# Cross-attention's exponentials one step later, last feed-forward group by token halves, gate tile of 32 columns

## The reference, cut to what matters

```
proj = h @ w_in                       # mixer; g_low has 16 columns
log_g = log_sigmoid(g_low @ gk_w2 + gk_b) / 16

q = (h @ wq).reshape(b, s, 4, 256)    # cross-attention, 4 heads
kv = mem_n @ wkv
scores = einsum('bshd,bmhd->bhsm', q, k) * 256 ** -0.5
probs = softmax(scores)
o = einsum('bhsm,bmhd->bshd', probs, v) ;  return o @ wo

u = conv3(h @ w_up) ; return (silu(gate) * val) @ w_down
out = rms_norm_2(x, norm_final_w)
```

## Time and profile before

| | us |
|---|---|
| median of 3 runs | 2532.43 (2531.82 to 2532.86) |
| profiled execution, whole time | 2531.77 |
| its span, first to last instruction | 2530.2 |
| PE busy | 2472.4 (98%) |
| DVE busy | 1397.4 (55%) |
| ACT busy | 792.6 (31%) |
| POOL busy | 79.1 (3%) |

### The profile page before, as it was taken

One profiled execution on the slowest core, in us unless ns is written; L12 is line 12 of the kernel. 1 busy time (PEld: TensorE's weight loads), 2 busy tenths in 40 slices (PEclk: granted clock), 3 DMA queues, 4 the chain that ended last, 5 costly groups with the idle time before them and its releaser, 6 DMA issues.

```text
span 2530.2 us, 31908 instructions
## 1 busy us (share of the span) xinstructions
PE 2472.4 (98%) x11704; PEld 2047.4 (81%) x11704; DVE 1397.4 (55%) x2254; ACT 792.6 (31%) x1473; POOL 79.1 (3%) x90
## 2 busy tenths in 40 slices
PE   8999999999999999999999999999999999999997
PEld 6868888888788878788788888888888888888886
DVE  5537788777542242335454753463687347734763
ACT  4234444454531121222232242453232112211223
POOL 1000000000000000021000030002000000000000
PEclk9999999999999999999999999999999999999998
DMA  5111111111111131221110042461111111111112
GB/s 194 42 33 42 51 42 51 50 44 57 48 44 50 50 108 50 78 80 55 34 50 21 26 143 63 136 196 50 42 50 50 50 50 50 42 49 50 50 46 79
DMA packets 236688, 157.75 MB, mean 62 GB/s; under 512 B 5087, under 2 KB 225396, under 8 KB 235075
## 3 DMA queue, kind: packets, MB, share of 16 engines
q1 hardware_dynamic: 231632, 133.71, 17.9%
q0 software_dynamic: 3088, 14.54, 1.6%
q10 hardware_dynamic: 1890, 8.43, 1.0%
HBM read 135.69 MB, written 20.97 MB: 62 GB/s over the span
## 4 chain that ended last, share of the span: by engine, by line
PE 92%; DVE 3%; ACT 2%; DMA 1%; issue 1%; SPq 0%; ACTq 0%; DVEq 0%
PE bank L698 27%; PE bank L699 27%; PE bank L700 27%; PE bank L990 1%; PE bank L832 1%; PE bank L991 1%; PE bank L992 1%; DMA wraw<-in_w_in_dram 1%; PE bank L843 1%; ACT whi L1199 1%; PE bank L794 1%; PE bank L844 1%; PE bank L822 1%; PE bank L821 1%; DVE wlo L1694 1%
## 5 line engine op out<-in xcount | busy, mean ns | idle before, releaser
L698 PE MATMUL bank<-xhi,whi 128*128 128x512 f32 x1056 | 413.1, 391 | 3.9 <-issue 1.9
L699 PE MATMUL bank<-xlo,whi 128*128 128x512 f32 x1056 | 412.3, 390 | 0.0
L700 PE MATMUL bank<-xhi,wlo 128*128 128x512 f32 x1056 | 412.1, 390 | 0.0
L1694 DVE TENSOR_TENSOR wlo<-wraw,whi 128x1024 fp32r<-128x1024 f32 (+1 forms) x233 | 276.8, 1188 | 183.8 <-ACT whi L1199 131.1
L1206 ACT ACTIVATE whi<-wraw 128x1024 fp32r<-128x1024 f32 x142 | 150.0, 1056 | 616.9 <-PE bank L700 611.1
L698 PE MATMUL bank<-x4hi,whi 128*128 128x512 f32 x704 | 274.4, 390 | 0.0
L700 PE MATMUL bank<-x4hi,wlo 128*128 128x512 f32 x704 | 274.0, 389 | 0.0
L699 PE MATMUL bank<-x4lo,whi 128*128 128x512 f32 x704 | 274.0, 389 | 0.0
L698 PEld LDWEIGHTS bank<-xhi,whi 128*128 128x128 f32 x1056 | 198.9, 188 | 46.6 <-issue 2.2
L699 PEld LDWEIGHTS bank<-xlo,whi 128*128 128x128 f32 x1056 | 199.0, 188 | 41.7 <-issue 0.2
L700 PEld LDWEIGHTS bank<-xhi,wlo 128*128 128x128 f32 x1056 | 198.9, 188 | 41.5
(11 more groups left out here) (375 smaller groups left out, 4366.0 us busy)
## 6 DMA issues: line engine op xcount, KB each, us to landing
wraw<-in_w_in_dram SPq DMA_DIRECT2D x85, 512.0 KB, 3.9
wraw<-in_ffn_w_up_dram SPq DMA_DIRECT2D x44, 512.0 KB, 3.8
wraw<-in_xattn_wkv_dram SPq DMA_DIRECT2D x16, 512.0 KB, 3.9
wraw<-in_ffn_w_down_dram SPq DMA_DIRECT2D x16, 512.0 KB, 3.9
xraw<-in_x_dram SPq DMA_DIRECT2D x4, 1024.0 KB, 10.4
x_spill<-xt SPq DMA_DIRECT2D x8, 512.0 KB, 2.8
conv_spill<-tv POOLq DMA_DIRECT2D x8, 512.0 KB, 3.1
wraw<-in_w_attn_out_dram SPq DMA_DIRECT2D x8, 512.0 KB, 3.9
```

The source lines that it names most:

```text
L698: pe.matmul(acc, whi[slot][:, k, :], xh, start=(k == 0), stop=False)
L699: pe.matmul(acc, whi[slot][:, k, :], xl, start=False, stop=False)
L700: last = pe.matmul(acc, wlo[slot][:, k, :], xh, start=False, stop=(k == k_tiles - 1))
L1694: dve.tensor_tensor(wlo[slot][:, 0:n, :], wraw[slot][:, 0:n, :], whi[slot][:, 0:n, :].bitcast(F32), ALU.subtract).then_inc(s_wlo, 1)
```

## The change

Three edits, which share the counting of tiles.

1. Cross-attention. All q and k tiles are run ahead (X_DENSE = 16, in the order q q q, then k k q four times, then q). The 16 v and o tiles follow, two in unit 0, one in each of units 1 to 14, none in 15; o tiles are numbered by `VO` (head, half), those of half 0 are n = 0, 1, 3, 5. ACT and DVE run `x_exps(u-1)` and `x_normalise(u-1)` after the tiles of unit u. For k and v the copy comes before the split, for o the split before the copies. `store_vo` of tile t-3 stands before the load of t. The Exp table is loaded ahead by a one-column activation.
2. The last feed-forward group runs 16 passes: for each token half the 8 tiles again, each loaded and split again, 18 matmuls per pass; half 0 is normed and stored while half 1 runs.
3. Tile T_GL: the stationary operand is 32 columns wide, 16 of the high part beside 16 of the low part, so that two matmuls do what three did; `gkw` has its 16 rows twice and sums the two.

```diff
-for _n in range(5):
-    X_TILES += [("k", _n), ("q", 3 + _n)]
+for _n in range(4):
+    X_TILES += [("k", 2 * _n), ("k", 2 * _n + 1), ("q", 3 + _n)]
+X_TILES += [("q", 7)]
...
+X_TILES += [("v", 0), ("v", 1), ("o", 0), ("v", 2), ("v", 3), ("o", 1), ("v", 4), ("o", 2), ("v", 5), ("o", 3),
+            ("v", 6), ("o", 4), ("v", 7), ("o", 5), ("o", 6), ("o", 7)]
+VO = ((0, 0), (1, 0), (0, 1), (2, 0), (1, 1), (3, 0), (2, 1), (3, 1))
+X_GROUPS = [(X_DENSE, X_DENSE + 2)] + [(X_DENSE + 2 + _n, X_DENSE + 3 + _n) for _n in range(14)]
+X_GROUPS += [(len(X_TILES),) * 2]
...
             for j in range(len(X_TILES) + KT):
                 t = T_XQ + j
-                kind, n = X_TILES[j - 4] if j < len(X_TILES) + 4 else ("", 0)
-                if j >= 4 and kind == "o":
-                    store_vo(t - 4, n)
+                kind, n = X_TILES[j - 3] if 3 <= j < len(X_TILES) + 3 else ("", 0)
+                if kind == "o":
+                    store_vo(t - 3, n)
...
                     for m in range(2):
-                        sp.wait_ge(s_vo_stored[m], 64 if f < 4 else 128)
+                        sp.wait_ge(s_vo_stored[m], (32, 96)[m] if f < 4 else 128)
                     load(t, t % 2, vo_spill[:, f, :, :])
...
+            loads(t, 8, (w, 0, 2), (w, 1, 2))
...
+                    for n, x in enumerate((x2hi, x2lo)):
+                        last = pe.matmul(ps(2 * slot + h)[0:32, :], whi[slot][:, k, 0:32],
+                                         x[:, k, h * HALF:(h + 1) * HALF], start=(k + n == 0),
+                                         stop=(k + n == KT))
...
+            for n in range(2 * KT):
+                t, h = T_LAST + n, n // KT
+                slot = t % 2
+                pe.wait_ge(s_wlo, t + 1)
+                pe.wait_ge(s_free, 2 * t - 2)
+                for k in range(FF_GROUPS[-1]):
+                    if n % KT == 0:
+                        pe.wait_ge(s_ffn_lo, 2 * (FF_TILES - FF_GROUPS[-1] + k) + h + 1)
...
+                last.then_inc(s_acc, 2)
+                if n:
+                    turn_result(n - 1)
+            turn_result(2 * KT - 1)
...
                 if kind == "k":
-                    split(t + 2, slot)
                     act.wait_ge(s_acc, 2 * t + 2)
                     act.activation(mkhi[:, n, :], ps(2 * slot)[:, 0:MEM], ACT.Copy).then_inc(s_mem_k_hi_ready, 1)
+                    split(t + 2, slot)
...
                 if kind == "o":
+                    split(t + 2, slot)
                     act.wait_ge(s_free, 2 * t)
...
-                    split(t + 2, slot)
...
+            act.activation(idle_act[:, 0:1], eps[:, :], ACT.Exp)
...
-                if u >= 2:
+                if u == 4 * XHEADS - 1:
                     x_turned_hi(u - 2)
-                x_exps(u)
-                if u % 4 == 3:
-                    x3_back(u // 4)
+                if u:
+                    x_exps(u - 1)
+                if 2 <= u < 4 * XHEADS - 1:
+                    x_turned_hi(u - 2)
+                if u % 4 == 0 and u:
+                    x3_back(u // 4 - 1)
+            x_exps(4 * XHEADS - 1)
+            x3_back(XHEADS - 1)
...
+                if n == KT + 1:
+                    result_root(0)
+                if n == KT + 2:
+                    result_norm(1)
+                if n == KT + 3:
+                    result_norm(3)
+            square_result(2 * KT - 1)
+            result_root(1)
+            result_norm(5)
+            result_norm(7)
...
+                if isinstance(t, int) and t == T_GL:
+                    dve.tensor_tensor(whi[slot][:, :, 16:32], wraw[slot][:, :, 0:16],
+                                      whi[slot][:, :, 0:16].bitcast(F32), ALU.subtract).then_inc(s_wlo, 1)
+                    return
...
             for u in range(4 * XHEADS):
+                for j in range(*X_GROUPS[u]):
+                    x_tile(j)
+                if u == 4 * XHEADS - 1:
+                    x_turned_lo(u - 2)
+                x_maxima(u)
                 if u:
                     x_normalise(u - 1)
-                for j in range(*X_GROUPS[u]):
-                    x_tile(j)
-                x_maxima(u)
-                if u >= 2:
+                if 2 <= u < 4 * XHEADS - 1:
                     x_turned_lo(u - 2)
...
+            for n in range(2 * KT):
+                h, f = n // KT, n % KT
+                tt, sl = T_LAST + n, (T_LAST + n) % 2
+                dve.wait_ge(s_acc, 2 * tt + 2)
+                r = resid[:, f, h * HALF:(h + 1) * HALF]
+                dve.tensor_tensor(r, ps(2 * sl + h), r, ALU.add).then_inc(s_free, 2)
+                if n + 2 < 2 * KT:
                     split(tt + 2, sl)
```

More of the change, by code:

```diff
@@ L250, in hybrid_then_mixer_kernel @@
         ghalf = at("gate_half", [P, HALF], F32, TMP + 12 * S)
-        glow = at("gate_low", [16, S], F32, B)
-        gkw = at("gk_w2", [16, 2 * P], F32, B + 4 * S)
+        glow = at("gate_low", [32, S], F32, B)
+        gkw = at("gk_w2", [32, 2 * P], F32, B + 4 * S)
         phi = at("pool_hi", [P, 4, S], F32R, C)
@@ L660, in _ @@
             pool.wait_ge(s_acc, 2 * T_P)
-            pool.dma_start(gkw[:, :], gk_w2_2[0]).then_inc(s_gk_loaded, 16)
+            for n in range(2):
+                pool.dma_start(gkw[16 * n:16 * n + 16, :], gk_w2_2[0]).then_inc(s_gk_loaded, 16)
             for f in range(KT):
@@ L668, in _ @@
                 sum_squares(3, f, f % 2)
-            pool.wait_ge(s_acc, 2 * (T_END - KT))
+            pool.wait_ge(s_acc, 2 * T_LAST)
             pool.dma_start(gfin[:, :], norm_final_w_2.rearrange("(a d) -> a d", a=1).broadcast_to([P, D]))\
@@ L1168, in _, with turn_result @@
                 t += 8
[L1169 to L1175, removed]
-                    for j in range(4):
-                        b = 4 * c + j
-                        last = pe.transpose(ps(4 + n % 4)[:, j * P:(j + 1) * P], resid[:, f, b * P:(b + 1) * P],
-                                            ident[:, :])
-                    last.then_inc(s_ft, 1)
-            for f in range(KT):
-                dense(t + f, (t + f) % 2, fhi, flo, k_tiles=FF_GROUPS[-1],
-                      ready=lambda k, h: (s_ffn_lo, 2 * (done - FF_GROUPS[-1] + k) + h + 1))
-                if f:
-                    turn_result(f - 1)
-            turn_result(KT - 1)
+            def turn_result(n):
+                h, f = n // KT, n % KT
+                pe.wait_ge(s_free, 2 * (T_LAST + n) + 2)
+                if n >= 4:
+                    pe.wait_ge(s_fc, n - 3)
+                for j in range(HB):
+                    b = HB * h + j
+                    last = pe.transpose(ps(4 + n % 4)[:, j * P:(j + 1) * P], resid[:, f, b * P:(b + 1) * P],
+                                        ident[:, :])
+                last.then_inc(s_ft, 1)
+            for n in range(2 * KT):
[6 more added lines that the diff above has]
+                        pe.wait_ge(s_ffn_lo, 2 * (FF_TILES - FF_GROUPS[-1] + k) + h + 1)
+                    xh, xl = fhi[:, k, h * HALF:(h + 1) * HALF], flo[:, k, h * HALF:(h + 1) * HALF]
+                    pe.matmul(ps(2 * slot + h), whi[slot][:, k, :], xh, start=(k == 0), stop=False)
+                    pe.matmul(ps(2 * slot + h), whi[slot][:, k, :], xl, start=False, stop=False)
+                    last = pe.matmul(ps(2 * slot + h), wlo[slot][:, k, :], xh, start=False,
+                                     stop=(k == FF_GROUPS[-1] - 1))
+                last.then_inc(s_acc, 2)
+                if n:
+                    turn_result(n - 1)
+            turn_result(2 * KT - 1)
         @block.scalar
```

146 lines of the change are left out of this document (81 added, 65 removed).

## The result

The kernel after the change takes 2540.01 us (median of 8 runs, 2537.93 to 2542.33) beside 2532.35 us for the kernel before (8 runs, 2530.84 to 2532.86): ratio 1.0032, interval 1.0022 to 1.0041. It is slower, by 7.7 us. The prediction was 2528.9 us, and it was wrong: 2540.0 lies outside its range (2518.5 to 2535). The profiled execution after took 2540.96 us with a span of 2539.4.

A forecast was written before the change was run, and what follows sets the result against it. TensorE, busy 2472.4 of 2530.2 us, was taken as the bound. Cross-attention +3.9, gate tile -1.4 and last group -6.0 summed to -3.5: 2528.3 us profiled, 2528.9 us as median of runs, range 2518.5 to 2535.

The forecast's parts named there:

- What goes: Cross-attention: with exponentials one step later, PE's six idle gaps close, -8.2 us (bounds 0 to -8.2).
- (a): Cross-attention's dense k, k, q order: q's split is late by 0.41 us four times, +1.6 us.
- (b): Cross-attention, SP's queue: stores ahead of the load three tiles on, mostly hidden, +0.6 us (bounds 0 to +5).
- rival (3): Slower through DMA landings L: above 4.3 us each adds 5(L - 4.3) at o0 to o4, 3L - 11.4 at the end; chance 0.07.
- (c): Cross-attention's end: first output-projection load waits for the store of unit 12's tile; PE waits 3.9 and 4.4 us, +8.3 us.
- (d): Cross-attention's clock: one stretch of 3.2 us at half speed after (c)'s second gap, +1.6 us (bounds 0 to +4).
- Gate tile, -1.4: Gate stage: 48 matmuls become 32, but the fifth pool matmul waits for DVE's scaling; -1.4 us (bounds -1.0 and -3.6).
- Last group, +1.7 - 7.7 = -6.0: Last feed-forward group: last matmul 1.7 us later at the start wait, tail 7.7 us shorter; -6.0 us.
- Faster 0.43: Chance of over 0.2% faster: no end waits, only one of the two, or a quarter of the forecast.
- slower 0.07: Whole kernel: chance of being slower by over 0.2%, from landings of 5.25 us or more.
- the forecast's own (0.59): Whole kernel: chance given to the forecast itself, a change of -8 to +2 us.

The follow-up runs named there:

- e8: Changed kernel with the earlier order of v and o tiles, and each unit's last split behind copies, exponentials and normalising: 2514.9 us against 2531.33, ratio 0.994.
- e7: Changed kernel with the two stores of each mem_v_out tile issued by GpSimd instead of SP: 2524.2 us against 2531.33, ratio 0.9973.
- e5: Changed kernel with the earlier order of v and o tiles, half 0 of vo complete two units earlier: 2539.0 us against 2531.33, ratio 1.0035.
- e11: Changed kernel with both the tile order of e5 and the GpSimd stores of e7: 2518.79 us against 2531.78, ratio 0.9955.
- e1: Kernel before with the 32-column gate tile alone: 2528.68 us against 2531.24, ratio 0.9994.
- e4: Kernel before with the gate tile and the last group by halves, cross-attention as before: 2523.05 us, ratio 0.9966.
- e2: Kernel before with the last feed-forward group by token halves alone: 2525.2 us, ratio 0.9981.

## Why the prediction was wrong, point by point

**What goes, -8.2: right.** e8 shows -8.1 with PE dense: PE's own work is longer than ACT's and DVE's, as the prediction worked out from the earlier trace rows.

**(a) k, k, q, +1.6: wrong, 0.** Its lower bound came: PE has no gap ahead of q3 to q6. The profile after, at the second k tile of the pair ahead of q4:

```profile
1552.50 1.05 ACT L1223 ACTIVATE whi<-wraw 128x1024 fp32r<-128x1024 f32 x1
1553.58 1.22 DVE L1741 TENSOR_TENSOR wlo<-wraw,whi 128x1024 fp32r<-128x1024 f32 x1 [0.45 <-ACT whi L1223]
1554.89 0.47 PE L704 MATMUL bank<-x3hi,whi 128*128 128x512 f32 x1
```

VectorE is done at 1554.80, 0.09 us ahead of PE's next start: in time. The prediction added a restart of 0.43 us that a row shows only where PE had waited; here it hadn't.

**(b) SP's queue, +0.6: the step that failed.** Measured 9.3 us by starts, restarts included: 1.7 by the load behind o0's stores, then 3.3, 1.3 and 3.0 by those behind o1's, o2's and o3's. The links that it lists are the right ones, and so is the price that rival (3) put on them: landings above 4.3 us cost 5(L - 4.3), and the ring's threshold is 4.28. What was wrong is L. The sum took 3.9, the median of the k and v loads of the kernel before, most of which go out alone. In the ring a load goes out within 0.5 us of two stores of 256 KB, and it took 4.92 us behind o0, 5.67 behind o2 and 5.47 behind o4, and 7.39 and 7.55 behind o1 and o3, where x3_back's 1 MB was issued within a microsecond as well. (A second load follows 0.6 to 2.1 us later each time, so the runs don't say what each neighbour costs.) For the ring's three full turns, landing minus 4.28 gives 3.11 + 1.39 + 3.27 = 7.8 us, and the three gaps add up to 7.6; the 1.2 us of o4 show no gap of their own, they delay the copies that (c)'s store waits for. So rival (3) is what came. It had been given 0.07 on the ground that the earlier trace rows have medians of 3.5 to 3.9, rows of the order before, where copies left early and the stores stood a tile further off: the median of a queue that the change rearranges. The trace did hold the landings of crowded stretches, up to 6.2 (a store) and 5.8 (a load).

A second fault lies beside it: (b) followed one tile from its end to its load and called the lateness slack that is used once. It didn't ask whether the load that is late delays the copies that the next load stands behind. It does: the load behind o2's stores goes out 5.9 us after the tile's end (1644.95 to 1650.81), not 2.8, since in ScalarE the copies stood behind a split whose weight landed only at 1645.73. So the lateness isn't forgiven at the next unit but carried on.

**(c) The end, +8.3: right in kind, measured 11.2** (7.6 and 3.6 by starts, predicted 3.9 and 4.4). The loads landed as taken (3.64 and 4.35 us); the store did not: 7.79 us (1684.37) where 3.4 had been put. x3_back was issued 0.1 us ahead of it, and the store 0.5 us earlier still landed in 2.87. The estimate by the Trainium skill ("DMA: Bandwidth & Descriptors", "Anatomy of one DMA — SWDGE (gpsimd) path": a fixed part of about 2.0 us plus bytes at 436 GB/s, which the section gives for DMAs that GpSimd issues, where these are SP's), 2.6 us for the store, was still further off. That a load behind a fresh store comes after two landings, e7's chain bears out (7.12 and 3.70 us). The order of tiles that removes it brought nothing that can be measured in e5 (1.0035 against 1.0032), where it made the ring costlier; with the stores out of SP's queue it is worth 5.2 us of cross-attention (e7 209.3, e11 204.1).

**(d) The clock, +1.6: measured 5.7 us,** 1.4 behind the gap that ends at 1671.33 (12 matmuls of the scores took 2.73 us, at full clock 1.44) and 4.3 behind the last two, which lie in one stretch of half clock. The prediction had one such stretch behind (c)'s second gap; it came already with the first, and one more behind o3. It isn't a matter of the gap's length alone: behind 2.86 us (1647.95) the granted clock was 1.00, behind 2.79 us (1671.33) it was 0.50. (The expectation of e5 puts some 0.5 us of this into the second end gap: 4.1 there, and 5.3 for the clock.)

Cross-attention then is -8.1 + 0 + 9.3 + 11.2 + 5.7 = +18.1, and 18.3 were measured.

**Gate tile, -1.4: right;** -1.7 in the traces after, of e1 and of e4, while e1's -2.6 us by medians has an interval that reaches from -4.0 to +0.8. The gap at the fifth pool matmul is where it was put (the line's number is now L909):

```profile
1219.67 3.67 PE L909 MATMUL bank<-pool,pool_w 128*128 128x512 f32 x8 [1.56 <-DVE pool L2086]
```

**Last group, +1.7 - 7.7 = -6.0: right** in both terms (+1.9, -7.7), and e2 measures -6.0. The tail after, which answers the earlier trace rows:

```profile
2527.42 0.60 PE L1192 MATMUL bank<-ident,resid 128*128 128x128 f32 x4
...
2531.67 2.19 ACT L1685 ACTIVATE y<-y,out_inverse 128x1024 f32<-128x1024 f32 x2 [0.24 <-DVE out_inverse L2436]
2532.45 2.88 SPq L583 DMA_DIRECT2D out_dram<-y  x4
```

Norms 4.25 us after the last dense matmul (predicted 4.3), first store 5.03 (5.1), end of the span 11.94 (12.0). There is no table load behind the last dense matmul.

**The chances.** Faster 0.43 and slower 0.07 had their weights on (c) alone: whether its waits came or not. The likeliest way to the other side was landing times in a queue that the change itself rearranges, and every term of the sum that holds a landing, (b) and (c), moves with it; such a common factor wants a chance like the forecast's own (0.59), not about a tenth of it.

## What to carry to other kernels

When an edit moves a load's consumer ahead of the work whose result a store waits for, and stores and loads share an in-order queue, write the ring out (landing + split + copies + store issue) and compare one turn with the bottleneck engine's work between two turns: a turn that is longer is paid again each time. Take landing times from stretches as crowded as the changed queue will be, not from a median over the kernel. And put work that a store needs ahead of work that itself waits for a load: here, with the stores three tiles on, that order of two lines was worth 20 us.

## What the runs showed of the hardware

A 512 KB load takes 3.9 us (median of the k and v loads before) where most go out alone. In the kernel after it took 4.9 to 5.7 us right behind two 256 KB stores, and 7.4 to 7.6 with a 1 MB load issued beside them as well, each time with a second 512 KB load close behind, while the second half of cross-attention as a whole moves only 148 GB/s. A 256 KB store issued 0.1 us after the 1 MB load took 7.79 us, against a median of 3.2 in the same stages of the kernel before. Late landings alone cost PE nothing where no load stood behind a store in the queue: e7 has loads of 7.5 and 7.9 us in stretches without a gap.

The half clock at 1366 to 1374 in the kernel before doesn't come in every execution, though the code of that stage is the same: in the stretch 1362 to 1380 the granted clock of the profiled executions was 0.72 in e1, 0.81 in e4 and 1.00 in e2. The stage was 4.4 us shorter in the profiled execution after than in that of before, and the clock is the difference that the rows show; a comparison of two single executions can err by as much.
